# A decoder step's second expert tables: table tiles stationary, tokens moving, and sums that need no turning back

## The chip, the core and the metric

The kernel is one program on one core of a Trainium2 chip. Its time is the device time of one execution in microseconds; the median of several executions is compared. The core has TensorE (matrix products into PSUM), VectorE, ScalarE, GpSimd and the DMA queue of SyncE, each with its own in-order program; they meet through semaphores.

## What is computed

One inference step of a small two-layer decoder, for 256 prompt tokens and 8 x 4 sample tokens, 1024 features. Layer 0 mixes tokens by gated linear attention, layer 1 by a recurrent block. Each is followed by a PEER channel mixer: every token picks 128 of 16384 single-neuron experts (8 heads, top 16 each):

```python
x = x + g1 * mixed
hm = rms_norm(x, p['norm_ffn_g'][i]) * (1 + sc2) + sh2
x = x + g2 * peer_mixer(hm, ...)
...
act = gelu(einsum('thkd,td->thk', u_tab[idx], xb))
wgt = g * act
return einsum('thk,thkd->td', wgt, v_tab[idx])
```

A final norm gives y. Outputs also include the mixers' new states.

## The kernel before

For the prompt tokens the kernel doesn't gather experts. It multiplies with both whole tables, in 128 tiles of 128 experts, and makes the weight of an expert that a token didn't pick zero. Activations lie turned: features on partitions, tokens along the free dimension (`x`, `x2`, `hid`: 128 partitions x 8 feature tiles kk x 288 tokens, the first 256 of the prompt). The 32 sample tokens do gather their rows (`picked`, GpSimd's indirect DMA); their weighted sum `mix_acc` is turned by eight small matmuls (L1469) into bank 3 of `pu`.

Precision comes from splitting each operand into a rounded high and a low part, both fp32r, and adding three products: high x high, high x low, low x high. A table tile comes by DMA from the SyncE queue into one of four slots of `raw`; ScalarE rounds it into `w_hi` (`high`, L814), VectorE (or GpSimd in the U stage) makes `w_lo` (`low`, L1793). `w_hi` and `w_lo` have two buffers each, so the rounding of tile c waits until TensorE is done with tile c-2 (`split_used`). The DMA into a slot waits until the low part that reads it is done.

PEER of a layer has these stages: query projection, scores, routing on VectorE; **U**, the first tables, tile by tile into one of four banks of `pu` (`u_early` for 64 tiles, `u_late` for 64; L1380, L1381, L1385), where a 128x128 piece of the table is the stationary operand and 256 tokens move, 24 matmuls a tile; then **V**, the second tables (`v_four`, L1456 to L1458). In V, ScalarE rounds also the tile's weights of 256 tokens (`weight_high`, L975, into `hid_lo[:, s]`), VectorE makes their low part (`weight_low`, L2085, `hid_lo[:, 4 + s]`).

V before: the weights of 128 tokens are the stationary operand and 512 features of the table move. Two token blocks and two feature halves fill the four banks of `pm`; all 128 tiles add up there. So the result has tokens on partitions, and has to be turned back. Behind the last tile:

```python
for half in range(2):                                # ScalarE; VectorE takes the other banks (L2154)
    act.wait_ge(v_bank, lay * 3 + 2 * half + 1)
    act.activation(v_tok_out[:, 2 * half, :], pm[:, 2 * half, :], ACT.Copy).then_inc(v_evac_act, 1)
```

ScalarE copies banks 0 and 2 (L1041), VectorE banks 1 and 3 (L2154) to `v_tok_out`; TensorE turns them with 16 transposes of 128x128 (L1480) into `pu`; VectorE adds each feature tile, times the layer's gate, to `x2` (L2157) and signals `x_ready`. The sample part of `x` is computed ahead of that (L2146, L2148).

What follows V: in layer 0, ScalarE first rounds the first two weight tiles of the recurrent block's projection (`next_high`, the second waits for V's last tile), then takes squares of the eight tiles of `x` (`square`, L868); VectorE makes the two low parts; GpSimd adds squares in three pairs (0,1), (2,3), (4,5) (`fold_squares`, L596); TensorE sums pairs and the tiles 6 and 7 over partitions with `ones` (`square_sum`, L1263); then come conditioning sums (`gap_sums`, L1281) on TensorE, while the norm is applied elsewhere, and the projection. In layer 1 the squares start at once, and the final norm ends the kernel. Projections take three products in the order hi, hi, lo with 288 moving tokens (`three`, L1243 to L1245).

Of the kernel before, what the change touches and what calls it, by code (L numbers as in the profile page):

```python
# [20 lines left out]
ALU = mybir.AluOpType  # L21
ACT = mybir.ActivationFunctionType
AX_X = mybir.AxisListType.X

P = 128
D = 1024
KD = D // P
SEQ = 256
# [121 lines left out]
def build_step(nc, xt, ct, par, con, ada, gla_in, w_lr, w_gate2, gla_out, wq, keys, u_tab, u_rows, v_tab, rg_in, gates,  # L150
               rg_out, rg_tail, gla_state, h_state, conv_state,
               y_out, gla_p_out, gla_s_out, h_out, conv_p_out, conv_s_out):
    with ExitStack() as ctx:
        def sb(name, shape, dt=F32):
            return ctx.enter_context(nc.sbuf_tensor(name, shape, dt))

        def sem(name):
            return ctx.enter_context(nc.semaphore(name))
# [3 lines left out]
        hid_hi, hid_lo = hid_split[:, 0:KD, :], hid_split[:, KD:2 * KD, :]  # L162
        raw = sb("raw", [P, RING, D])
        w_hi = sb("w_hi", [P, 2, D], F32R)
        w_lo = sb("w_lo", [P, 2, D], F32R)
# [5 lines left out]
        mod = sb("mod", [P, 2, 6, KD, NSEQ])  # L171
# [9 lines left out]
        def area(at, *dims, dt=F32, parts=P):  # L181
            n = 1
            for d in dims:
                n *= d
            v = arena[0:parts, at:at + n]
            if dt != F32:
                v = v.bitcast(dt)
            if len(dims) == 2:
                return v.rearrange("p (a b) -> p a b", a=dims[0])
            if len(dims) == 3:  # L190
                return v.rearrange("p (a b c) -> p a b c", a=dims[0], b=dims[1])
            return v
# [5 lines left out]
        x2 = area(0, KD, T)  # L198
        x = area(34560, KD, T)
# [73 lines left out]
        part_d = [area(27648 + SLOTS * n, SLOTS) for n in range(3)]  # L273
        twice = [w.bitcast(F16).rearrange("p (n d) -> p n d", d=2) for w in part_d]
        pick_u, pick_g, pick_wa, sum4 = [ada_row[:, n * PICKS:n * PICKS + PICKS] for n in range(4)]
        def v_turned(kk):

            return pu[:, kk % 4, kk // 4 * SEQ:kk // 4 * SEQ + SEQ]

        v_tok_out = area(4096, 4, 512)  # L280

        def pcol(name, a=0, b=None):
            lo, hi = PAR_COLS[name]
# [2 lines left out]
        def ccol(name, parts=P):  # L286
            lo, hi = CON_COLS[name]
            return const[0:parts, lo:hi] if hi <= 2 * P else const_gla[0:parts, lo - 2 * P:hi - 2 * P]

        ident, iota = ccol("ident"), ccol("iota")  # L290


        pu = ctx.enter_context(nc.psum_tensor("pu", [P, 4, 512], F32))
        pm = ctx.enter_context(nc.psum_tensor("pm", [P, 4, 512], F32))
# [39 lines left out]
        x_ready = sem("x_ready")  # L334
# [11 lines left out]
        preset = sem("preset")  # L346
        o_turned = [pm[:, 2, :], pm[:, 3, :], pu[:, 2, :], pu[:, 3, :]]
        v_bank = sem("v_bank")
        v_evac_act = sem("v_evac_act")
        v_evac_vec = sem("v_evac_vec")  # L350
        v_turn = sem("v_turn")
        s_mix = sem("s_mix")
        xs_ready = sem("xs_ready")
        picked_in = [sem(f"picked_in{b}") for b in range(GRING)]
# [408 lines left out]
        def _(act):  # L763
# [88 lines left out]
            def root_table(out=mean[:, T - 1:T]):  # L852

                act.activation(out, pcol("final_g", 0, 1), ACT.Abs_reciprocal_sqrt)
# [46 lines left out]
            def peer(lay):  # L901
# [128 lines left out]
                for c in range(NKEY):  # L1030
# [5 lines left out]
                        act.activation(sp[:, 1, :], sp[:, 1, :], ACT.Exp, scale=-1.0).then_inc(lame_ready, 1)  # L1036
                    if c == NKEY - 2:
                        root_table(sel_w[:, 0:1])
                for half in range(2):
                    act.wait_ge(v_bank, lay * 3 + 2 * half + 1)  # L1040
                    act.activation(v_tok_out[:, 2 * half, :], pm[:, 2 * half, :], ACT.Copy).then_inc(v_evac_act, 1)  # L1041


            act.wait_ge(x_in, 16)
# [58 lines left out]
            for j in range(24):  # L1103
# [4 lines left out]
                if j in MIX_ROW:  # L1108
                    g, half = MIX_ROW[j]
# [39 lines left out]
            norm_root(1)  # L1149
            norm_high(1, 0, 3)  # L1150
            peer(0)


# [74 lines left out]
            act.wait_ge(mod_ready, 11)  # L1228
            norm_high(3, 1, 3)
            peer(1)  # L1230
            for kk in range(KD):
                square(4, kk)
# [4 lines left out]
        def _(pe):  # L1237
            mm = pe.matmul

            def three(out, cols, kk, r_hi, r_lo, s, n_k, stop=True):  # L1240
                s2 = s % 2

                mm(out, w_hi[:, s2, cols], r_hi, start=(kk == 0), stop=False)  # L1243
                mm(out, w_hi[:, s2, cols], r_lo, start=False, stop=False)  # L1244
                return mm(out, w_lo[:, s2, cols], r_hi, start=False, stop=(stop and kk == n_k - 1))  # L1245
# [96 lines left out]
            def peer(lay):  # L1342
# [6 lines left out]
                for n in range(9):  # L1349
# [4 lines left out]
                    if n < 8:  # L1354
                        for a in range(4):
                            hp = 4 * (n % 4) + a
                            last = mm(pm[:, n % 4, a * P:a * P + P], qp[:, hp, (n // 4) * P:(n // 4) * P + P], key[:, hp, :],  # L1357
                                      start=True, stop=True)
                    else:
                        for hp in (4 * g + a for a in range(4) for g in range(4)):  # L1360
                            at = hp // 4 * 32
                            last = mm(pm[at:at + 32, 0, (hp % 4) * P:(hp % 4) * P + P], qp[:, hp, SEQ:T], key[:, hp, :],
                                      start=True, stop=True)
# [84 lines left out]
                def v_four(i, first=False, final=False):  # L1448
                    for s in range(4):
                        pe.wait_ge(lo_done, i * 4 + (l0 + NKEY - POOL_ALL + s + 1))  # L1450
                        pe.wait_ge(w_ready, i * 4 + (n0 + s + 1))
                        start, stop = first and s == 0, final and s == 3
                        for bank in range(4):
                            out, cols = pm[:, bank, :], slice(bank // 2 * 512, bank // 2 * 512 + 512)
                            tok = slice(bank % 2 * P, bank % 2 * P + P)
                            mm(out, hid_lo[:, s, tok], w_hi[:, s % 2, cols], start=start, stop=False)  # L1456
                            mm(out, hid_lo[:, 4 + s, tok], w_hi[:, s % 2, cols], start=False, stop=False)  # L1457
                            last = mm(out, hid_lo[:, s, tok], w_lo[:, s % 2, cols], start=False, stop=stop)  # L1458
                            if stop and bank < 3:
                                last.then_inc(v_bank, 1)  # L1460
                        last.then_inc(split_used, 1)

                v_four(0, first=True)
                with pe.Fori(1, NKEY // 4 - 1) as i:
                    v_four(i)
                pe.wait_ge(mix_added, (lay + 1) * (PICKS - 1))
                pe.wait_ge(u_prod, (lay + 1) * LATE)
                for kk in range(KD):
                    last = mm(pu[:, 3, kk * 32:kk * 32 + 32], mix_acc[:, kk * P:kk * P + P], sum4, start=True, stop=True)  # L1469
                last.then_inc(s_mix, 1)  # L1470
                v_four(NKEY // 4 - 1, final=True)
                pe.wait_ge(xs_ready, lay + 1)
                for half in range(2):
                    pe.wait_ge(v_evac_act, 2 * lay + half + 1)
                    pe.wait_ge(v_evac_vec, 2 * lay + half + 1)
                    for a in range(4):
                        if half:
                            pe.wait_ge(x_ready, (2 * lay + 1) * KD + a + 1)
                        for tb in range(2):
                            last = pe.transpose(v_turned(half * 4 + a)[:, tb * P:tb * P + P],  # L1480
                                                v_tok_out[:, half * 2 + tb, a * P:a * P + P], ident)
                        last.then_inc(v_turn, 1)


            pe.wait_ge(ones_set, 1)
# [161 lines left out]
            for j in range(24):  # L1647
# [11 lines left out]
                for kk in range(KD):  # L1659
                    if j == 0:  # L1660
                        pe.wait_ge(hl_ready, kk + 1)
                    last = three(pu[:, j % 2, 0:T], slice(kk * P, kk * P + P), kk, hid_hi[:, kk, :], hid_lo[:, kk, :], j, KD)
# [5 lines left out]
            for c in range(KD):  # L1668
# [3 lines left out]
                for kk in range(KD):  # L1672
                    if c == 0:
                        pe.wait_ge(hl_ready, LOW_BEFORE["gla_out"] + kk + 1)
                    last = three(pu[:, c % 4, 0:T], slice(kk * P, kk * P + P), kk, hid_hi[:, kk, :], hid_lo[:, kk, :], c, KD)
# [12 lines left out]
            for g in (5, 6):  # L1688
                gap_sums(g)
            peer(0)  # L1690


# [49 lines left out]
            for o in range(KD):  # L1742
# [11 lines left out]
                for e in range(2):  # L1754
                    last = mm(pu[:, o % 4, 0:T], tail[:, e, o * P:o * P + P], yb[:, KD + e, :], start=False, stop=(e == 1))
# [5 lines left out]
            pe.wait_ge(mod_ready, 11)  # L1761
            gap_sums(11)
            peer(1)
            pe.wait_ge(ones_set, 3)
            for kk in range(KD):
# [4 lines left out]
        def _(dve):  # L1770
            own = [0]
            tt_, ts, stt = dve.tensor_tensor, dve.tensor_scalar, dve.scalar_tensor_tensor
# [228 lines left out]
            def peer(lay):  # L2001
# [144 lines left out]
                link(tt_(part.rearrange(by_seq, b=NB), pu[:, 3, 0:256].rearrange("p (k b t) -> p k b t", k=KD, b=NB),  # L2146
                         bc(mod[:, lay, 5, :, 1:NSEQ], P, KD, NB, NT), ALU.mult))
                tt_(x[:, :, SEQ:T], x2[:, :, SEQ:T], part, ALU.add).then_inc(xs_ready, 1)  # L2148
                for half in range(2):
                    if half == 0:  # L2150
                        dve.wait_ge(v_bank, lay * 3 + 2)
                    else:
                        dve.wait_ge(split_used, m0 + 2 * NKEY)
                    dve.tensor_copy(v_tok_out[:, 2 * half + 1, :], pm[:, 2 * half + 1, :]).then_inc(v_evac_vec, 1)  # L2154
                for kk in range(KD):
                    dve.wait_ge(v_turn, lay * KD + kk + 1)
                    stt(x[:, kk, 0:SEQ], v_turned(kk), mod[:, lay, 5, kk, 0:1], x2[:, kk, 0:SEQ], ALU.mult,  # L2157
                        ALU.add).then_inc(x_ready, 1)


# [135 lines left out]
            state_sample(5, pm[:, 2:4, :])  # L2296
            out_rows("gla_out", 1, 0, 2)
            peer(0)


# [94 lines left out]
            dve.tensor_copy(hl_out[:, :, 1:NSEQ], samples(g_r)[:, :, :, NT - 1]).then_inc(hs_ready, 1)  # L2395
            out_rows("rg_out", 3, 1, 2)
            peer(1)
            norm_inverse(4)
            for kk in range(KD):
# [94 lines left out]
```

## Time and profile before

| | us |
|---|---|
| median of 3 runs | 2035.35 (2032.27 to 2035.69) |
| profiled execution | 2030.94 |
| its span | 2029.1 |
| TensorE busy, by the records | 1985.0 (98%), 14082 matmuls |
| weight loads on TensorE | 1761.6 (87%) |
| VectorE | 1401.7 (69%) |
| ScalarE | 1254.9 (62%) |
| GpSimd | 846.8 (42%) |

Busy shares are means over the whole span. PE is TensorE's matmuls, PEld its weight loads (they overlap), DVE is VectorE, ACT ScalarE, POOL GpSimd. Matmuls are pipelined and their ends are modelled: the pace of a stream of them is read from the starts. PEclk is the clock granted to TensorE, 1.00 being 2.4 GHz.

### The profile page before, as it was taken

The page shows a single profiled execution, that of the slowest core. Times are in us where ns is not written, and L with a number is a line of the kernel's source. Part 1 is how long each engine was busy: PE and PEld are TensorE (multiplying, and loading weights), DVE is VectorE, ACT ScalarE, POOL GpSimd, SP SyncE. Part 2 cuts the span into 40 slices and gives each one's busy share as a digit, 9 for nine tenths or more (in the row PEclk, how much of TensorE's full clock was granted, in tenths as well). Part 3 has the DMA queues.
Part 4 walks back from the last instruction along what each step waited for, and adds up shares of the span by engine and source line. Part 5 has one row for each costly group of instructions (what it writes and reads, how often), then busy time and mean ns, then how long its engine had stood idle before and what let it go on. Part 6 is the DMA issues. An engine that isn't in the chain of part 4 may idle for free.

```text
span 2029.1 us, 40794 instructions
## 1 busy us (share of the span) xinstructions
PE 1985.0 (98%) x14082; PEld 1761.6 (87%) x14082; DVE 1401.7 (69%) x2784; ACT 1254.9 (62%) x2212; POOL 846.8 (42%) x465
## 2 busy tenths in 40 slices
PE   7999999999999999999999999999999999999998
PEld 4778899999999877777778889999999997777776
DVE  3436569955666777777766754997566667777785
ACT  3544465556777677677654644655677776767774
POOL 0011037885777322234212411888477742223330
PEclk8999999999999999999999999999999999999999
DMA  9847755665455689988947554666655458888883
GB/s 352 294 167 272 266 177 171 186 212 172 155 156 157 204 290 320 351 311 328 326 148 245 166 200 136 186 184 189 198 156 157 157 167 306 297 300 292 301 291 115
DMA packets 125466, 459.54 MB, mean 226 GB/s; under 512 B 14016, under 2 KB 14544, under 8 KB 124352
## 3 DMA queue, kind: packets, MB, share of 16 engines
q1 hardware_dynamic: 103408, 378.71, 56.6%
q0 software_dynamic: 21072, 77.95, 10.5%
q10 hardware_dynamic: 896, 1.76, 0.2%
q8 instruction: 46, 0.75, 0.2%
q14 instruction: 44, 0.36, 0.1%
HBM read 449.93 MB, written 8.44 MB: 226 GB/s over the span
## 4 chain that ended last, share of the span: by engine, by line
PE 91%; DVE 4%; DMA 2%; ACT 1%; issue 1%; SPq 0%; POOL 0%; DVEq 0%; ACTq 0%
PE pu L1385 12%; PE pu L1380 12%; PE pm L1456 12%; PE pm L1458 12%; PE pm L1457 12%; PE pu L1381 12%; PE pu L1243 4%; PE pu L1244 4%; PE pu L1245 4%; PE pm L1415 3%; PE pm L1725 1%; DVE w_lo L1793 1%; DMA arena<-in_ada 1%; DMA raw<-in_gla_out 1%; PE pm L1357 1%; ACT w_hi L814 1%
## 5 line engine op out<-in xcount | busy, mean ns | idle before, releaser
L814 ACT ACTIVATE w_hi<-raw 128x1024 fp32r<-128x1024 f32 x600 | 633.1, 1055 | 410.1 <-PE pm L1458 220.1
L1793 DVE TENSOR_TENSOR w_lo<-raw,w_hi 128x1024 fp32r<-128x1024 f32 x372 | 458.3, 1232 | 365.2 <-ACT w_hi L814 348.9
L1380 PE MATMUL pu<-hid_split,w_hi 128*128 128x256 f32 x2048 | 492.2, 281 | 0.0
L1381 PE MATMUL pu<-hid_split,w_hi 128*128 128x256 f32 x2048 | 491.2, 279 | 0.0
L1456 PE MATMUL pm<-w_hi,hid_split 128*128 128x512 f32 x1024 | 403.9, 394 | 2.6 <-DVE hid_split L2085 2.6
L1458 PE MATMUL pm<-w_lo,hid_split 128*128 128x512 f32 x1024 | 402.3, 393 | 0.0
L1457 PE MATMUL pm<-w_hi,hid_split 128*128 128x512 f32 x1024 | 401.7, 392 | 0.0
L1380 PEld LDWEIGHTS pu<-hid_split,w_hi 128*128 128x128 f32 x2048 | 385.9, 188 | 0.8 <-issue 0.8
L1381 PEld LDWEIGHTS pu<-hid_split,w_hi 128*128 128x128 f32 x2048 | 385.1, 188 | 0.0
L660 POOL TENSOR_TENSOR w_lo<-raw,w_hi 128x1024 fp32r<-128x1024 f32 x128 | 306.4, 2394 | 152.8 <-ACT w_hi L814 152.8
L632 POOL TENSOR_TENSOR w_lo<-raw,w_hi 128x1024 fp32r<-128x1024 f32 x104 | 249.6, 2401 | 169.8 <-ACT w_hi L814 169.8
L1385 PE MATMUL pu<-hid_split,w_lo 128*128 128x256 f32 x2048 | 295.4, 287 | 0.0
L1385 PEld LDWEIGHTS pu<-hid_split,w_lo 128*128 128x128 f32 x2048 | 260.6, 189 | 0.2 <-POOL w_lo L632 0.2
L1456 PEld LDWEIGHTS pm<-w_hi,hid_split 128*128 128x128 f32 x1024 | 192.2, 188 | 70.3 <-issue 19.3
L1243 PE MATMUL pu<-hid_split,w_hi 128*128 128x288 f32 x736 | 227.5, 309 | 13.2 <-DVE w_lo L1793 5.6
L1458 PEld LDWEIGHTS pm<-w_lo,hid_split 128*128 128x128 f32 x1024 | 192.4, 188 | 43.6
L951 ACT ACTIVATE oh_w<-oh_eq,sel_w 128x128 f16<-128x128 f16 x512 | 163.9, 391 | 103.7 <-PE pm L1415 103.7
L1457 PEld LDWEIGHTS pm<-w_hi,hid_split 128*128 128x128 f32 x1024 | 192.7, 188 | 33.4
L1244 PE MATMUL pu<-hid_split,w_hi 128*128 128x288 f32 x736 | 219.7, 299 | 0.0
L1245 PE MATMUL pu<-hid_split,w_lo 128*128 128x288 f32 x736 | 218.9, 297 | 0.0
L647 POOL DMA_INDIRECT arena<-in_v_tab,coef x64 | 110.0, 1719 | 219.5 <-DVE arena L2111 174.4
L647 POOL DMA_INDIRECT arena<-in_u_rows,coef x64 | 76.2, 1191 | 237.4 <-ACT arena L1002 235.9
(283 smaller groups left out, 2559.0 us busy)
## 6 DMA issues: line engine op xcount, KB each, us to landing
raw<-in_u_tab SPq DMA_DIRECT2D x256, 512.0 KB
raw<-in_v_tab SPq DMA_DIRECT2D x256, 512.0 KB
arena<-in_ada SPq DMA_DIRECT2D x56, 512.0 KB, 6.5
raw<-in_wq SPq DMA_DIRECT2D x32, 512.0 KB
raw<-in_gla_in SPq DMA_DIRECT2D x24, 512.0 KB
raw<-in_ada SPq DMA_DIRECT2D x24, 512.0 KB
raw<-in_rg_in SPq DMA_DIRECT2D x20, 512.0 KB
arena<-in_ada SPq DMA_DIRECT2D x8, 1024.0 KB, 16.7
```

The source lines that it names most:

```text
L660: pool.tensor_tensor(w_lo[:, c % 2, :], raw[:, slot, :], w_hi[:, c % 2, :].bitcast(F32), ALU.subtract).then_inc(lo_pool, 1)
L814: act.activation(w_hi[:, s2, :], raw[:, s4, :], ACT.Copy).then_inc(hi_done, 1)
L1243: mm(out, w_hi[:, s2, cols], r_hi, start=(kk == 0), stop=False)
L1244: mm(out, w_hi[:, s2, cols], r_lo, start=False, stop=False)
L1245: return mm(out, w_lo[:, s2, cols], r_hi, start=False, stop=(stop and kk == n_k - 1))
L1380: mm(pu[:, s, 0:SEQ], w_hi[:, s % 2, kk * P:kk * P + P], hid_hi[:, kk, 0:SEQ], start=(kk == 0), stop=False)
L1381: mm(pu[:, s, 0:SEQ], w_hi[:, s % 2, kk * P:kk * P + P], hid_lo[:, kk, 0:SEQ], start=False, stop=False)
L1385: last = mm(pu[:, s, 0:SEQ], w_lo[:, s2, kk * P:kk * P + P], hid_hi[:, kk, 0:SEQ], start=False, stop=(kk == KD - 1))
L1456: mm(out, hid_lo[:, s, tok], w_hi[:, s % 2, cols], start=start, stop=False)
L1457: mm(out, hid_lo[:, 4 + s, tok], w_hi[:, s % 2, cols], start=False, stop=False)
L1458: last = mm(out, hid_lo[:, s, tok], w_lo[:, s % 2, cols], start=False, stop=stop)
L1793: tt_(w_lo[:, s2 if l2 is None else l2, :], raw[:, s4, :], w_hi[:, s2, :].bitcast(F32), ALU.subtract).then_inc(lo_done, 1)
```

## The change

In V the operands change places. A 128x128 piece of the table tile becomes the stationary operand and the 256 tokens' weights move. Each of the eight feature tiles kk has a sum of its own of 128 features x 256 tokens; two of them share a bank of `pm`. Per tile there are 24 matmuls of 256 columns where there were 12 of 512. The first matmul of a bank starts it; the second sum of the bank begins on cleared columns.

The result has features on partitions, as `x` does. `v_tok_out`, its four evictions, the 16 transposes and three semaphores go; VectorE's residual operations read the sums in `pm`: kk 0 to 5 after their bank is complete (`v_bank`), 6 and 7 after the last tile. TensorE's wait for `xs_ready` goes too.

```diff
-        def v_turned(kk):
-            return pu[:, kk % 4, kk // 4 * SEQ:kk // 4 * SEQ + SEQ]
-        v_tok_out = area(4096, 4, 512)
+        def v_sum(kk):
+            return pm[:, kk // 2, kk % 2 * SEQ:kk % 2 * SEQ + SEQ]
...
-                for half in range(2):
-                    act.wait_ge(v_bank, lay * 3 + 2 * half + 1)
-                    act.activation(v_tok_out[:, 2 * half, :], pm[:, 2 * half, :], ACT.Copy).then_inc(v_evac_act, 1)
...
-                        for bank in range(4):
-                            out, cols = pm[:, bank, :], slice(bank // 2 * 512, bank // 2 * 512 + 512)
-                            tok = slice(bank % 2 * P, bank % 2 * P + P)
-                            mm(out, hid_lo[:, s, tok], w_hi[:, s % 2, cols], start=start, stop=False)
-                            mm(out, hid_lo[:, 4 + s, tok], w_hi[:, s % 2, cols], start=False, stop=False)
-                            last = mm(out, hid_lo[:, s, tok], w_lo[:, s % 2, cols], start=False, stop=stop)
-                            if stop and bank < 3:
+                        for kk in range(KD):
+                            out, cols = v_sum(kk), slice(kk * P, kk * P + P)
+                            mm(out, w_hi[:, s % 2, cols], hid_lo[:, s, 0:SEQ], start=(start and kk % 2 == 0), stop=False,
+                               skip_group_check=True)
+                            mm(out, w_hi[:, s % 2, cols], hid_lo[:, 4 + s, 0:SEQ], start=False, stop=False,
+                               skip_group_check=True)
+                            last = mm(out, w_lo[:, s % 2, cols], hid_lo[:, s, 0:SEQ], start=False, stop=stop,
+                                      skip_group_check=True)
+                            if stop and kk in (1, 3, 5):
                                 last.then_inc(v_bank, 1)
                         last.then_inc(split_used, 1)
...
-                pe.wait_ge(xs_ready, lay + 1)
-                for half in range(2):
-                    pe.wait_ge(v_evac_act, 2 * lay + half + 1)
-                    pe.wait_ge(v_evac_vec, 2 * lay + half + 1)
-                    for a in range(4):
-                        if half:
-                            pe.wait_ge(x_ready, (2 * lay + 1) * KD + a + 1)
-                        for tb in range(2):
-                            last = pe.transpose(v_turned(half * 4 + a)[:, tb * P:tb * P + P],
-                                                v_tok_out[:, half * 2 + tb, a * P:a * P + P], ident)
-                        last.then_inc(v_turn, 1)
...
-                for half in range(2):
-                    if half == 0:
-                        dve.wait_ge(v_bank, lay * 3 + 2)
+                for kk in range(KD):
+                    if kk < KD - 2:
+                        dve.wait_ge(v_bank, lay * 3 + kk // 2 + 1)
                     else:
                         dve.wait_ge(split_used, m0 + 2 * NKEY)
-                    dve.tensor_copy(v_tok_out[:, 2 * half + 1, :], pm[:, 2 * half + 1, :]).then_inc(v_evac_vec, 1)
-                for kk in range(KD):
-                    dve.wait_ge(v_turn, lay * KD + kk + 1)
-                    stt(x[:, kk, 0:SEQ], v_turned(kk), mod[:, lay, 5, kk, 0:1], x2[:, kk, 0:SEQ], ALU.mult,
+                    stt(x[:, kk, 0:SEQ], v_sum(kk), mod[:, lay, 5, kk, 0:1], x2[:, kk, 0:SEQ], ALU.mult,
                         ALU.add).then_inc(x_ready, 1)
```

## Rows read from the trace of the kernel before

**Rows 1.** The page: TensorE's busy time, and the chain by engine

```profile
PE 1985.0 (98%) x14082; PEld 1761.6 (87%) x14082; DVE 1401.7 (69%) x2784; ACT 1254.9 (62%) x2212; POOL 846.8 (42%) x465
...
PE 91%; DVE 4%; DMA 2%; ACT 1%; issue 1%; SPq 0%; POOL 0%; DVEq 0%; ACTq 0%
```

**Rows 2.** Windows: length; busy PE, PEld, DVE, ACT, POOL; PEclk, DMA share, GB/s

```profile
684.90:1041.80 356.90, 356.89 (x1554) 284.38 (x1555) 275.41 (x346) 244.08 (x359) 92.46 (x65) 1.00 0.86 305
...
1658.05:2014.80 356.75, 356.74 (x1554) 284.44 (x1555) 271.89 (x323) 242.55 (x355) 89.52 (x62) 1.00 0.80 275
...
1264.00:1439.00 175.00, 175.00 (x1495) 175.00 (x1494) 149.61 (x474) 99.02 (x150) 137.04 (x57) 1.00 0.62 191
```

**Rows 3.** Timeline of PE, layer 0: V's first matmul, its 1488th (start, duration)

```profile
684.91 0.47 PE L1456 MATMUL pm<-w_hi,hid_split 128*128 128x512 f32 x1 [1.31 <-DVE hid_split L2085]
...
1028.50 0.39 PE L1458 MATMUL pm<-w_lo,hid_split 128*128 128x512 f32 x1
```

**Rows 4.** Groups by line: busy us, mean ns of one, then idle before

```profile
L1385 PEld LDWEIGHTS pu<-hid_split,w_lo 128*128 128x128 f32 x2048 | 260.6, 189 | 0.2 <-POOL w_lo L632 0.2
...
L2157 DVE SCALAR_TENSOR_TENSOR arena<-pu,mod,arena 128x256 f32<-128x256 f32 x16 | 6.4, 474 | 0.0
```

**Rows 5.** Timeline of a V tile in layer 0: rounding, low part, first load

```profile
851.30 0.40 PE L1456 MATMUL pm<-w_hi,hid_split 128*128 128x512 f32 x1
...
851.50 1.06 ACT L814 ACTIVATE w_hi<-raw 128x1024 fp32r<-128x1024 f32 x1 [1.44 <-PE pm L1458]
...
852.59 1.23 DVE L1793 TENSOR_TENSOR w_lo<-raw,w_hi 128x1024 fp32r<-128x1024 f32 x1 [0.72 <-ACT w_hi L814]
...
853.94 0.19 PEld L1456 LDWEIGHTS pm<-w_hi,hid_split 128*128 128x128 f32 x1 [0.17 <-issue]
854.03 0.41 PE L1456 MATMUL pm<-w_hi,hid_split 128*128 128x512 f32 x1
```

**Rows 6.** Timeline of PE, U stage of layer 1: first matmuls of tiles 22 apart

```profile
1332.23 0.28 PE L1380 MATMUL pu<-hid_split,w_hi 128*128 128x256 f32 x1
...
1394.12 0.28 PE L1380 MATMUL pu<-hid_split,w_hi 128*128 128x256 f32 x1
```

**Rows 7.** Timeline of PE in the last query projection, 12 matmuls apart

```profile
1229.87 0.30 PE L1243 MATMUL pu<-hid_split,w_hi 128*128 128x288 f32 x1
...
1231.47 0.30 PE L1243 MATMUL pu<-hid_split,w_hi 128*128 128x288 f32 x1
```

**Rows 8.** Timeline of the end of V and what follows, layer 0

```profile
1038.96 0.42 DVE L2148 TENSOR_TENSOR arena<-arena 128x256 f32<-128x256 f32 x1
...
1041.41 0.40 PE L1458 MATMUL pm<-w_lo,hid_split 128*128 128x512 f32 x1
...
1041.63 2.00 ACT L814 ACTIVATE w_hi<-raw 128x1024 fp32r<-128x1024 f32 x2
...
1043.53 2.76 ACT L868 ACTIVATE arena<-arena 128x288 f32<-128x288 f32 x8
...
1044.38 3.28 POOL L596 TENSOR_TENSOR arena<-arena 128x288 f32<-128x288 f32 x3 [6.34 <-ACT arena L868]
...
1047.71 1.72 PE L1263 MATMUL pm<-arena 128*128 128x288 f32 x6 [0.98 <-POOL arena L596]
```

**Rows 9.** Timeline of the end of V and what follows, layer 1

```profile
2014.44 0.39 PE L1458 MATMUL pm<-w_lo,hid_split 128*128 128x512 f32 x1
...
2015.48 3.22 DVE L2157 SCALAR_TENSOR_TENSOR arena<-pu,mod,arena 128x256 f32<-128x256 f32 x8
...
2016.90 2.36 POOL L596 TENSOR_TENSOR arena<-arena 128x288 f32<-128x288 f32 x3 [7.46 <-ACT arena L868]
...
2017.85 3.19 PE L1263 MATMUL pm<-arena 128*128 128x288 f32 x10 [0.23 <-POOL arena L596]
```

**Rows 10.** Timeline of PE in a U tile of layer 1: neighbours

```profile
1357.67 0.27 PE L1381 MATMUL pu<-hid_split,w_hi 128*128 128x256 f32 x1
1357.78 0.28 PE L1380 MATMUL pu<-hid_split,w_hi 128*128 128x256 f32 x1
```

More of the change, by code:

```diff
@@ L348, in build_step @@
         v_bank = sem("v_bank")
-        v_evac_act = sem("v_evac_act")
-        v_evac_vec = sem("v_evac_vec")
-        v_turn = sem("v_turn")
         s_mix = sem("s_mix")
```

## The prediction

> **What bounds the kernel now.** I read the page first. TensorE is busy 98% of the span, and the chain that ended last is 91% TensorE [rows 1]. In such a kernel a change of shape on TensorE counts in full, unless something else already held it there. So I cut the trace into stretches. The two V stages (the second tables) are the ones the change touches: 684.9 to 1041.8 and 1658.05 to 2014.8 us. TensorE is without a gap in both, its granted clock is 1.00 of the upper level (2.4 GHz), while VectorE, ScalarE and the DMA engines have room [rows 2].
>
> Then I looked for the pace. In a V stage 124 of the 128 table tiles run without a break: 1488 matmuls, the first starting at 684.91 and the last at 1028.50 [rows 3]. That is 343.59 us over 1487 steps, 231.1 ns from one 512-column matmul to the next, or 12 x 0.2311 = 2.773 us a tile. The duration beside each (0.47 and 0.39) isn't the pace, since matmuls overlap; only starts count.
>
> Is that pace TensorE's own? The double buffering makes a loop: the end of tile c-2 releases ScalarE's rounding of tile c, then VectorE's low part, then the first weight load. In one tile it reads: ScalarE 851.50, VectorE 852.59 to 853.82, load 853.94, matmul 854.03; the tile before had started at 851.30 [rows 5]. So the loop can't be shorter than 854.03 - 851.30 = 2.73 us a tile, and stands just 0.04 below TensorE's 2.773. TensorE bounds, with the loop close behind.
>
> **Part 1, the matmuls turned round.** Per tile, 12 matmuls of 512 columns with 12 loads become 24 of 256 columns with 24 loads. The columns streamed stay the same, 6144. What counts is what each matmul costs beyond its columns. The U stage of this kernel has nearly the wanted form: 24 matmuls a tile, a 128x128 piece of the table stationary, 256 tokens moving, w_hi twice and w_lo once per piece. From 1332.23 to 1394.12 it does 22 tiles at an even pace [rows 6]: 61.89 / 22 = 2.813 us, 117.2 ns a matmul. Two halves thus cost 234.4 where one whole costs 231.1. In the U stage the loads (188 ns each in the listing, [rows 4]) fill 175.00 of 175.00 us [rows 2], and still the matmuls keep 117.2 ns; so doubling the loads is hidden by the matmuls, for as long as loads go on beside them.
>
> Differences from U: V takes hi, hi, lo piece by piece, and leaves an accumulator after 3 matmuls and a bank after 6, where U does 16 and then 8 into one. Projections have that three-step order with 288 columns: from 1229.87 to 1231.47 there are 12 steps of 133.3 ns [rows 7]. At 2.4 GHz 288 columns are 120.0 ns, so 13.3 are overhead; 256 columns are 106.7, so U's overhead is 10.5. With 13.3 a V matmul would take 120.0 ns, a tile 2.88 us. If I draw a line through U's 256 columns and V's 512 instead, 288 columns would be 131.3 ns; the projections are only 2.0 over it. So the ends are 2.73 (the loop, if TensorE got cheaper) and 2.88 us. I take 2.82: U's pace plus a tenth of the way to the projections', because size and kind of the matmuls are U's. The step per tile is 2.82 - 2.773 = +0.047, over 127 tiles in each of two stages +11.9 us. The ends give -10.9 and +27.2. The loop is now 0.09 below TensorE and hides; SP's loads of table tiles wait for the low parts as before, and DMA moves the same bytes in a longer stage (busy 0.86 and 0.80 of it now [rows 2]).
>
> The Trainium skill (TensorE: Matmul & The Clock Gate, Back-to-back issue gap) has, for isolated matmuls, columns divided by 2.4 GHz plus 2.5 ns; an estimate by it is 24 x 109.2 - 12 x 215.8 = +31 ns a tile, +7.9 us in all. The trace has both a good deal dearer (117.2 and 231.1), with nearly the same difference, so the sum stays with the rows.
>
> **Part 2, the tail behind V.** Out go two ScalarE and two VectorE evictions, 16 transposes and their waits; the eight residual operations (474 ns each when not overlapped in the listing) read the bank sums directly. Six of them have their banks before V is over, 0.7 us apart; VectorE is free there, since its sample sums end at 1039.4 [rows 8]. Only kk 6 and 7 remain behind the last matmul, at about 0.05 and 0.5, ready by 1.0 us.
>
> After layer 1 the modelled end of V is 2014.44 + 0.39 = 2014.83, and the sum of squares is done at 2021.04 [rows 9]: 6.2 us. Afterwards: squares of kk 0 to 5 are done by +0.7, the last at +1.6 (eight take 2.76 in [rows 8]; 0.45 for one alone), GpSimd's third addition (2.36 / 3 = 0.8) at +1.5, then the last three sums on TensorE, 1.72 as in [rows 8]: +3.3. I save 2.9. The bounds: if only the stretch from 2014.83 to the first residual at 2015.48 came out, it were 0.65; if all of the residuals' 3.22 went with it too, 3.9.
>
> After layer 0 less comes free. ScalarE has two roundings of the next weights ahead of its squares, and the second needs the end of V: V + 0.02, 1.06 long. So squares run from about +1.1 rather than from 1043.53 - 1041.80 = +1.73, and this is what is late next. VectorE's two low parts, which run beside GpSimd's additions now (3.28 us for three against 2.36 without them [rows 8, 9]), mostly get out of their way. Additions end at about +4.5 for +5.86, the sums at +6.3 for 1049.43 - 1041.80 = +7.63. I save 1.5, within 0.6 and 2.2. The conditioning sums (gap sums 8 and 9) and the projection follow on TensorE in order and just move.
>
> **Sum.** +11.9 - 2.9 - 1.5 = +7.5 us. On the profiled execution (2030.94 us, span 2029.1, so 1.8 around it) that gives 2038.4. The timed runs stand at 2035.35, 4.4 above the profiled one, and the same step gives 2042.9. Their spread is 3.4 us, so 0.2% (4.1 us) is about what can be told from no change.
>
> **Rivals.**
> *About the same (0.17).* U's pace exactly (+10.2) or a bit under it, and tails at their best ends (-3.9 - 2.2 = -6.1): +4.1 or less, 2035 to 2039. For it: 2.813 is a row of this kernel; against: both must come out well.
> *The three-step order costs as in the projections (0.15).* Accumulator and bank change often and each matmul keeps 13.3 ns over its columns: +27.2 - 4.4 = +22.8, 2058. For it speak rows 7, against it that U differs from them in columns and in order alike.
> *Faster (0.08).* The turned matmuls cost less than U's. In a U tile some steps are only 0.11 us, as from 1357.67 to 1357.78, where both operands change [rows 10], and in V both change at a third of the steps or the destination does. If all 24 took 0.113, TensorE would want 2.71, the rounding loop would hold it at 2.73, and the time would be -10.9 - 4.4 = -15.3, 2020. It decides from under 2.790 us a tile (2.773 + 4.4/254); for a gain over 0.2% the tile must not be dearer than now, 2.774. Against it: all 24 steps average 117.2.
> *Weight loads set the pace (0.02).* Each 188 ns load stands unhidden ahead of its matmul: 24 x 0.188 = 4.51 us of loads alone, +1.74 a tile, +442 us, 2473. It needs that loads don't overlap with matmuls, and in the U stage they plainly do [rows 2, 6]. The same page and section of the Trainium skill says that the spacing in a stream of load and matmul pairs is set by both of them, with 131 ns for 512 columns; that rule speaks against halving the columns, but here 512 columns take 231.1 ns, so the trace doesn't bear its figure out.
>
> **How the numbers follow.** The forecast case has 0.58 and its own range is 2.81 to 2.85 us a tile with the tails' ends: 2038 to 2053. The range reaches down over most of the "same" case to 2034 and up to 2056, under the dear case's centre; outside are about 0.09 below and 0.1 above. A slowdown over 0.2% holds 0.56 of the forecast, and the dear and load cases: 0.73. Within 0.2%: 0.18. Faster: 0.09.
>
> **What would show it.** (a) V matmuls 117 to 119 ns apart, tiles 2.81 to 2.85: right; under 2.79 or over 2.86: my price was wrong. (b) V stages 6 us longer each, in which the idle time of VectorE and ScalarE grows. (c) The low part of a tile ends over 0.3 us ahead of the tile's first matmul; otherwise the loop bounds. (d) The residuals of kk 0 to 5 start before V's last matmul, two after it. (e) Squares' sums at about V's end +6.3 (layer 0) and +3.3 (layer 1). The prediction fails if the step from matmul to matmul depends on order and banks rather than on columns, for 1 ns a matmul is 6.1 us.

## The result, and the profile after

The changed kernel takes 2056.14 us (median of 4 runs, 2055.44 to 2057.37), the kernel before 2033.92, four runs as well: the ratio is 1.0111, interval 1.0097 to 1.0125, or +22.2 us. I had forecast +7.5 and a range up to 2056.0. The direction was right, the size was three times mine, and it ended just outside the range.

The page of the changed kernel, TensorE's busy time:

```profile
PE 2007.4 (98%) x17122; PEld 1929.1 (94%) x17122; DVE 1398.2 (68%) x2780; ACT 1253.2 (61%) x2208; POOL 852.0 (41%) x465
```

The windows of its V stages (columns as in [rows 2]):

```profile
688.80:1057.50 368.70, 368.52 (x3088) 368.35 (x3088) 277.00 (x351) 244.14 (x358) 94.94 (x65) 1.00 0.85 296
...
1675.40:2044.00 368.60, 368.52 (x3088) 368.34 (x3088) 273.40 (x328) 243.12 (x358) 92.37 (x63) 1.00 0.79 267
```

TensorE still has no gap and its clock is 1.00, but loads now fill the stage (368.35 of 368.70; 284.38 of 356.90 in [rows 2]). VectorE and ScalarE are about as busy as before, in a longer stage: they have more slack. So the added time is TensorE's own pace. The loop of rounding and low part isn't what holds it: in layer 0 a tile's low part ends 0.33 to 0.36 us before the tile's first matmul starts, as here (850.60 + 1.23 = 851.83, matmul 852.18).

```profile
850.60 1.23 DVE L1776 TENSOR_TENSOR w_lo<-raw,w_hi 128x1024 fp32r<-128x1024 f32 x1 [1.29 <-issue]
...
852.18 0.28 PE L1447 MATMUL pm<-hid_split,w_hi 128*128 128x256 f32 x1
```

The pace itself, first matmuls of tiles that are 64 apart in layer 0:

```profile
746.23 0.28 PE L1447 MATMUL pm<-hid_split,w_hi 128*128 128x256 f32 x1
...
929.49 0.28 PE L1447 MATMUL pm<-hid_split,w_hi 128*128 128x256 f32 x1
```

That is 183.26 / 64 = 2.863 us a tile, 119.3 ns a matmul, where I had taken 2.82. Now the end of V in both layers, from the timelines:

```profile
1055.31 3.23 DVE L2137 SCALAR_TENSOR_TENSOR arena<-pm,mod,arena 128x256 f32<-128x256 f32 x8 [0.48 <-PE pm L1451]
...
1057.13 0.28 PE L1451 MATMUL pm<-hid_split,w_lo 128*128 128x256 f32 x1
...
1058.41 2.76 ACT L863 ACTIVATE arena<-arena 128x288 f32<-128x288 f32 x8
1058.46 2.35 DVE L1776 TENSOR_TENSOR w_lo<-raw,w_hi 128x1024 fp32r<-128x1024 f32 x2
1059.25 3.84 POOL L591 TENSOR_TENSOR arena<-arena 128x288 f32<-128x288 f32 x3 [5.83 <-ACT arena L863]
...
1061.74 5.14 PE L1255 MATMUL pm<-arena 128*128 128x288 f32 x10 [4.33 <-POOL arena L591]
...
2043.72 0.28 PE L1451 MATMUL pm<-hid_split,w_lo 128*128 128x256 f32 x1
...
2044.28 3.19 PE L1255 MATMUL pm<-arena 128*128 128x288 f32 x10 [0.28 <-POOL arena L591]
```

In layer 1 the sum of squares ends at 2047.47, 3.75 us behind the start of V's last matmul; before it was 2021.04 - 2014.44 = 6.60 [rows 9]. In layer 0 it ends at 1066.88, 9.75 behind; before 1049.43 - 1041.41 = 8.02 [rows 8]. The tail with less work in it became longer. Two windows, the gap and the sums behind it, show one reason:

```profile
1057.40:1061.70 4.30, 0.01 (x1) 0.00 (x0) 3.55 (x6) 3.72 (x9) 2.45 (x2) 0.83 0.73 243
1061.70:1066.90 5.20, 5.16 (x14) 3.25 (x18) 0.00 (x0) 0.00 (x0) 1.40 (x2) 0.50 0.47 164
```

The transposes had stood in that gap. Without them TensorE sits idle for 4.33 us, and the granted clock falls to 0.50, the level of 1.2 GHz: ten records of sums take 5.14 us, for 1.42 + 1.72 before.

The account, from first to last matmul start: V in layer 0 went from 356.50 to 368.24 us, in layer 1 from 356.38 to 368.24, together +23.6; layer 0's tail +1.7; layer 1's tail -2.85. The sum is +22.5, for +22.2 in the medians. (The profiled execution is slower by 4.0 us more, ahead of V, where the code is the same; V begins anywhere from 683.6 to 689.0 in the traces of all kernels here that leave the U stage as it is.)

### The profile page after: what moved, and what is told of

It is laid out like the page before. It is cut to its first block, busy times and chain, and to the rows that moved or that the text cites. A ratio compares the mean times of both kernels' runs of the same rounds, so it can differ in the third digit from the quotient of the medians.

```text
span 2055.6 us, 46862 instructions
## 1 busy us (share of the span) xinstructions
PE 2007.4 (98%) x17122; PEld 1929.1 (94%) x17122; DVE 1398.2 (68%) x2780; ACT 1253.2 (61%) x2208; POOL 852.0 (41%) x465
## 4 chain that ended last, share of the span: by engine, by line
PE 90%; DVE 4%; DMA 3%; ACT 2%; issue 1%; SPq 0%; POOL 0%; DVEq 0%; ACTq 0%
PE pu L1377 12%; PE pm L1447 12%; PE pm L1451 12%; PE pm L1449 12%; PE pu L1372 12%; PE pu L1373 11%; PE pu L1235 4%; PE pu L1236 4%; PE pu L1237 4%; PE pm L1407 3%; PE pm L1708 1%; DVE w_lo L1776 1%; DMA arena<-in_ada 1%; DMA raw<-in_gla_in 1%; DMA raw<-in_gla_out 1%; PE pm L1349 1%
## 5 line engine op out<-in xcount | busy, mean ns | idle before, releaser
L1447 PE MATMUL pm<-hid_split,w_hi 128*128 128x256 f32 x2048 | 578.4, 282 | 2.6 <-DVE hid_split L2068 2.6
L1451 PE MATMUL pm<-hid_split,w_lo 128*128 128x256 f32 x2048 | 577.7, 282 | 0.0
L1449 PE MATMUL pm<-hid_split,w_hi 128*128 128x256 f32 x2048 | 577.7, 282 | 0.0
L1447 PEld LDWEIGHTS pm<-hid_split,w_hi 128*128 128x128 f32 x2048 | 389.0, 190 | 3.0 <-issue 3.0
L1449 PEld LDWEIGHTS pm<-hid_split,w_hi 128*128 128x128 f32 x2048 | 388.6, 190 | 0.0
L1451 PEld LDWEIGHTS pm<-hid_split,w_lo 128*128 128x128 f32 x2048 | 388.4, 190 | 0.0
L642 POOL DMA_INDIRECT arena<-in_v_tab,coef x64 | 114.6, 1791 | 226.0 <-DVE arena L2094 179.1
```

What stands on the lines that cost most here:

```text
L1447: mm(out, w_hi[:, s % 2, cols], hid_lo[:, s, 0:SEQ], start=(start and kk % 2 == 0), stop=False, skip_group_check=True)
L1449: mm(out, w_hi[:, s % 2, cols], hid_lo[:, 4 + s, 0:SEQ], start=False, stop=False, skip_group_check=True)
L1451: last = mm(out, w_lo[:, s % 2, cols], hid_lo[:, s, 0:SEQ], start=False, stop=stop, skip_group_check=True)
```

## The experiments

Unless said otherwise a time is from one profiled execution of each, and the pace is read from the V stage of layer 0: start of a tile's first matmul to that of a tile 64 later. Three things differ between the V matmuls (119.3 ns) and the U matmuls (117.2): order, destination, and what moves. The first four kernels take them, and the DMA traffic, one at a time.

**U's order in V.** All hi products of a tile, then all lo products:

```diff
                             mm(out, w_hi[:, s % 2, cols], hid_lo[:, 4 + s, 0:SEQ], start=False, stop=False,
                                skip_group_check=True)
+                        for kk in range(KD):
+                            out, cols = v_sum(kk), slice(kk * P, kk * P + P)
                             last = mm(out, w_lo[:, s % 2, cols], hid_lo[:, s, 0:SEQ], start=False, stop=stop,
                                       skip_group_check=True)
```

> The changed kernel with the 24 matmuls of a V tile in the order of the U stage: hi, hi for the eight pieces, then lo for the eight. The changed kernel has 119.4 ns from matmul to matmul, the U stage 117.2. Theory A (the order hi, hi, lo, with both operands changing at every third step, costs the 2.2 ns): 117.2 ns here, a tile 2.81 us, about 13 us less than the changed kernel. Theory B (leaving an accumulator and a bank costs): accumulators change oftener here, 16 times a tile, so 119.4 or more. Theory C (the moving operand is freshly written and changes from tile to tile, or other traffic): no change, 119.4.

Measured: 741.62 to 924.88 for 64 tiles, 2.863 us. Not the order. A side finding: here the banks get complete only in the last eight matmuls, so in layer 1 the residuals start at 2038.70 for a last matmul at 2039.09, TensorE waits 1.70 us for the first addition, and its ten records of sums take 4.59 us, for 3.19 in the changed kernel. The clock falls there too (0.73 over 2039.3 to 2045.7), and layer 1's tail is back at 6.6 us.

**One accumulator.**

```diff
-                            out, cols = v_sum(kk), slice(kk * P, kk * P + P)
+                            out, cols = v_sum(kk if first or final else 0), slice(kk * P, kk * P + P)
```

> The changed kernel, but in 120 of 128 V tiles all 24 matmuls add into one 256-column accumulator, so the sums of those tiles are wrong. Theory B (changing accumulators and banks costs the 2.2 ns): 117.2 ns a matmul. Theories A (order) and C (moving operand or traffic): 119.4 as in the changed kernel.

Measured: the V stage takes 368.23 us, as the changed kernel's 368.24. Neither accumulators nor banks matter.

**Other moving operands.** `hid_hi[:, kk]` and `hid_hi[:, (kk + 1) % KD]` in place of the two slots of weights.

> The changed kernel, but in 120 of 128 V tiles the moving operands are the still activations that the U stage streams (high parts, another feature tile at each piece) and not the tile's fresh weights; the sums of those tiles are wrong. Theory C1 (streaming a freshly written operand costs): 117.2 ns a matmul. Theories A, B and C2 (DMA traffic): 119.4.

Measured: 118.8 ns, a stage of 366.63 us. The first of the edits that moves the pace at all, but it doesn't reach 117.2. Both fresh data and the addresses changed here, and either could be what counts.

**Light DMA.** `raw[:, s, 0:256]` is loaded in V instead of the whole slot.

> The changed kernel, but the loads of table tiles in V bring 256 of 1024 columns (the rest of the slot keeps older values, so V's sums are wrong). The DMA engines' busy share in V falls from about 0.85 to 0.3 or less. Theory C2 (the heavier DMA traffic of V, 300 GB/s against 190 in U, costs the 2.2 ns): 117.2 ns or less. Theories A, B, C1: 119.4.

Measured: 368.24 us, to the hundredth. The busy share of DMA fell less than I had expected, to 0.57 (176 GB/s, window 700 to 1020). That is a fall by a third, to below the 0.62 and 191 GB/s of the U stage [rows 2], and it did nothing.

**V's addresses in the U stage.** The clean cross test: U streams `hid_lo[:, s]` and `hid_lo[:, 4 + s]`, which nobody writes there.

```diff
-   mm(pu[:, s, 0:SEQ], w_hi[...], hid_hi[:, kk, 0:SEQ], ...)
-   mm(pu[:, s, 0:SEQ], w_hi[...], hid_lo[:, kk, 0:SEQ], ...)
+   mm(pu[:, s, 0:SEQ], w_hi[...], hid_lo[:, s, 0:SEQ], ...)
+   mm(pu[:, s, 0:SEQ], w_hi[...], hid_lo[:, 4 + s, 0:SEQ], ...)
```

(and `hid_lo[:, s]` with `w_lo`.)

> The changed kernel with the U stage streaming the moving operands by V's addresses (one of four tiles of the low parts for the whole table tile, and one of the next four) in U's order; U's products are wrong. Theory M1 (addresses of the moving operand set the 2.2 ns between U and V): U rises from 117.2 to 119.4 ns, 2.81 to 2.86 us a tile. Theory E (V's surroundings, other engines' work, cost it): U stays at 117.2.

Measured: in its U stage of layer 1 the first matmuls of two tiles 18 apart start at 1366.39 and 1417.93. 51.54 / 18 = 2.863 us: U has taken on V's pace, in its own surroundings, with its own order and traffic, on data written long ago. What sets the difference is which addresses move.

**One moving tile.** All 24 matmuls stream `hid_hi[:, 0]`.

> The changed kernel, but in 120 of 128 V tiles all 24 matmuls stream one and the same activation tile (the sums of those tiles are wrong). With other activations moving the pace had fallen from 119.4 to 118.8 ns, and order, accumulators and DMA traffic had left it at 119.4 exactly. Theory M1 (the pace hangs on which addresses move beside which are loaded): it moves again, by 0.5 ns or more in either direction, and its pattern over the 24 steps differs. Theory E (what remains is other engines' work in the V stage): 118.8 to 119.4 with the pattern kept.

Measured: 744.50 to 928.82, 2.880 us a tile. All 24 steps are 120.0 ns, where the changed kernel has 119.3 on average with steps from 115 to 122. So the pace moved by 0.7 ns and the pattern is gone, as the address theory asked.

**Start addresses.** A slot is 288 floats, 1152 bytes, long: an odd multiple of 128. So slots start at even and odd multiples of 128 bytes by turns, counted from the tensor's start. In the changed kernel's trace the two kinds of tile differ: 2.873 us with even slots, 2.853 with odd. Shifting the 256 weights by 32 floats in every other slot makes all alike:

```diff
+        def w_at(k):
+            return hid_lo[:, k, 32 - 32 * (k % 2):32 - 32 * (k % 2) + SEQ]
```

used by ScalarE, VectorE and TensorE alike (`32 * (k % 2)` for all even).

> The changed kernel with the even slots of the tokens' weights shifted by 128 bytes, so that all eight moving slots begin at an odd multiple of 128 bytes; the result is the reference's. In the changed kernel tiles with even slots take 2.873 us and those with odd slots 2.853. Theory M2 (the start address of the moving operand sets that): all tiles 2.853, 2.5 us less in all. Rival H (the buffer of w_hi and w_lo, which alternates likewise, sets it): 2.873 and 2.853 stay.

> The changed kernel with the odd slots of the tokens' weights shifted by 128 bytes, so that all moving slots begin at an even multiple of 128 bytes from the tensor's start; the result is the reference's. All odd gave 2.848 us a tile for every slot. Theory M2 (the start address of the moving operand): 2.873 to 2.880 for every slot, 119.7 to 120.0 ns a matmul. Rival N (an alternating start is what costs, either uniform layout is cheap): 2.848.

The timelines, 64 tiles apart, all odd and then all even:

```profile
742.69 0.28 PE L1451 MATMUL pm<-hid_split,w_hi 128*128 128x256 f32 x1
...
924.96 0.28 PE L1451 MATMUL pm<-hid_split,w_hi 128*128 128x256 f32 x1
```

```profile
744.37 0.28 PE L1451 MATMUL pm<-hid_split,w_hi 128*128 128x256 f32 x1
...
928.69 0.28 PE L1451 MATMUL pm<-hid_split,w_hi 128*128 128x256 f32 x1
```

2.848 against 2.880 us, each the same for all four slots. The `w_hi` buffers alternate in both, so it isn't they. (The V stages are 366.28 and 370.37 us for the changed kernel's 368.24: all odd saves 3.9 us in both layers together, where I had expected 2.5.) The single moving tile above, `hid_hi[:, 0]`, starts at an even multiple and had the same 120.0 ns.

Still, 118.7 is not 117.2. U alternates both kinds of start, feature tile by feature tile, and does better than either alone. But mixing them is not enough: the kernel with other moving operands mixes them too, within each tile of V (even, odd, even, then odd, even, odd), and has 118.8; its tiles also take 2.844 and 2.856 us by turns, though all stream the same addresses. Which succession of addresses gives U its 117.2 stays open.

**The width.** The larger part is not 119 against 117, but 2 x 119 against 231. First the kernel before with its operands where they were and each matmul cut in two:

```diff
-   mm(out, hid_lo[:, s, tok], w_hi[:, s % 2, cols], ...)          # and the two others
+   for h in range(2):
+       o, cc = pm[:, bank, h * 256:h * 256 + 256], slice(cols.start + h * 256, cols.start + h * 256 + 256)
+       mm(o, hid_lo[:, s, tok], w_hi[:, s % 2, cc], ...)          # and the two others
```

> The kernel before, tokens stationary and its tail unchanged, with each 512-column matmul of V cut into two of 256 columns with a load each; the result is the reference's. Theory W (the width alone is the cost: half the columns, double the instructions and loads): 117 to 119.5 ns a matmul, the whole kernel 2035 + 10 to 23, as the changed kernel's V. Theory R (the changed roles of the operands cost): the pace stays at 231.1 / 2 = 115.6 ns, the time at 2035.

Measured: 742.72 to 925.75, 2.860 us a tile (119.2 ns), and 2054.95 us for the kernel, 22.6 over the 2032.34 of the kernel before beside it. Nothing was turned round here, and nearly the whole loss is there: the V stages take 367.81 us each, +22.7 in both layers together, for +23.6 in the changed kernel. Cutting a matmul in two also doubles the loads. No kernel here keeps one load for two halves, so what follows calls the two together the cost of the narrow matmul.

The other way: turned round, but with wide matmuls. The weights' high and low parts move together as 512 columns, 16 matmuls a tile.

```diff
+   both = hid_lo.rearrange("p (a b) t -> p b a t", a=2)[:, s, :, 0:SEQ]
+   mm(pm[:, kk // 2, :].rearrange("p (a t) -> p a t", a=2), w_hi[:, s % 2, cols], both, ...)
```

> The changed kernel, but in 120 of 128 V tiles the two products with the high table part are one 512-column matmul that streams the weights' high and low parts together, into a whole bank, so neighbouring sums mix and V is wrong: 16 matmuls and 16 loads a tile for 24, the same 6144 columns, the table still stationary. Theory W (a half-width matmul costs 3.8 ns more than half of a whole one): 231 + 119 ns per piece, a tile 2.80 us. Theory R (the table as the stationary operand costs, whatever the width): 2.86 us.

```profile
800.07 0.40 PE L1454 MATMUL pm<-hid_split,w_hi 128*128 128x512 f32 x1
800.31 0.28 PE L1456 MATMUL pm<-hid_split,w_lo 128*128 128x256 f32 x1
800.42 0.40 PE L1454 MATMUL pm<-hid_split,w_hi 128*128 128x512 f32 x1
```

Over 120 tiles a piece takes 232.8 + 118.8 ns and a tile 2.813 us: eight matmuls fewer, 51 ns less. The roles of the operands cost next to nothing (119.3 ns turned, 119.2 not turned), the narrow matmuls do.

**Narrower still**, 192 tokens in the inner tiles:

> The changed kernel, but in 120 of 128 V tiles only 192 of the 256 tokens move, so 64 tokens lack those tiles. Theory L (the stream of weight loads sets 119.4 ns, the columns hide behind it): still about 119 ns a matmul. Theory M (a matmul costs its columns at 2.4 GHz plus a fixed overhead of 12.7 ns): 80.0 + 12.7 = 92.7 ns, a tile 2.22 us, until ScalarE and VectorE bound it at 2.73 us a tile; then the matmuls within a tile still show 93.

Two neighbours within a tile are 112 ns apart, not 93. The window 700 to 1000 has the loads over the whole of it:

```profile
700.00:1000.00 300.00, 299.93 (x2663) 299.76 (x2662) 240.91 (x284) 216.63 (x316) 87.79 (x61) 1.00 0.92 330
```

A quarter fewer columns saved 7.3 of 119.3 ns where one column a cycle of 2.4 GHz would have saved 26.7. So at 192 columns something other than the columns sets the pace of a pair of load and matmul, and holds it at 112 ns. By the same estimate of one column a cycle, 256 columns (106.7 ns) pay 12.6 ns over their columns, or 25 for two, where 512 columns (213.3) pay 17.8. That 112 ns is a floor, near which 256 columns begin to pay, is my reading of these three widths; fewer than 192 columns weren't tried. (Tiles are 2.703 us there, 0.015 over 24 x 112 ns: the first step of a tile is 136 ns on average, the loop of rounding and low part showing, forecast at 2.73.) The Trainium skill (TensorE: Matmul & The Clock Gate, LDWEIGHTS (loading the stationary operand)) gives a load its columns divided by 1.2, an estimate of 107 ns for 128; the 112 ns from pair to pair lie close to it, but the record of one load in the changed kernel is 186 to 192 ns long, loads overlap, and these runs don't separate the load from other costs of a pair.

**The tail: clock.** 32 transposes of a constant on TensorE ahead of layer 0's sums.

```diff
+            for n in range(32):
+                pe.transpose(pu[:, n % 2, 0:P], ident, ident)
             pe.wait_ge(ones_set, 2)
```

> The changed kernel with 32 transposes of a constant on TensorE between layer 0's V and the sums of squares, where the 16 transposes stood before. In the changed kernel TensorE is idle there for 4.3 us, its granted clock is 0.50 behind it, and its ten records of sums take 5.14 us (1.42 + 1.72 with the clock at 1.00 before). Theory K (the idle time let the clock fall, and that ate the tail's gain): clock 1.00, the sums' end at about 7 us behind V's last matmul instead of 9.7, the kernel 2 to 3 us shorter there. Rival G (GpSimd's additions, 3.84 us for 3.28, are what is late, the clock is not the cause): the end moves by under 0.7 us.

```profile
1056.49 3.13 PE L1255 MATMUL pm<-arena 128*128 128x288 f32 x10 [0.83 <-POOL arena L591]
```

The clock is 1.00 over 1051.9 to 1059.6, and the sums end at 1059.62, 7.74 us behind the start of V's last matmul (1051.88), for 9.75. Theory K holds for 2.0 us. It only gives back what was lost: the tail before took 8.02.

**The tail: VectorE beside GpSimd.** In addition, the two low parts wait for the three additions (`dve.wait_ge(sq_added, FOLD_BEFORE[2] + 3)` ahead of `next_low`).

> The changed kernel with the 32 transposes of the warm-tail experiment, and VectorE's two low parts of the next weights moved behind GpSimd's three additions in layer 0. With the clock held at 1.00 the sums still ended 7.7 us behind V's last matmul, and the additions took 3.83 us, the first 2.4. Theory G (VectorE's low parts beside GpSimd's additions hold the first one up): three additions in 2.4 to 2.8 us, sums' end at 6.3 to 6.7 us behind the last matmul. Rival S (ScalarE's squares pace the additions): 3.8 us and 7.7 stay.

```profile
1057.21 0.28 PE L1451 MATMUL pm<-hid_split,w_lo 128*128 128x256 f32 x1
...
1059.35 2.31 POOL L591 TENSOR_TENSOR arena<-arena 128x288 f32<-128x288 f32 x3 [5.84 <-ACT arena L863]
...
1060.83 2.60 PE L1255 MATMUL pm<-arena 128*128 128x288 f32 x10
1061.68 2.36 DVE L1778 TENSOR_TENSOR w_lo<-raw,w_hi 128x1024 fp32r<-128x1024 f32 x2 [3.06 <-POOL arena L591]
```

The additions take 2.31 us for 3.83, and the sums end 6.22 behind the last matmul's start. Theory G holds for another 1.5 us. The next projection on TensorE starts 13.17 us behind V's last matmul, for 16.81 in the changed kernel and 14.97 before. (The whole kernels, one run each, took 2050.97 us with the transposes and 2054.26 with both; single runs differ by more than the 1.5 us.)

**The kernel before with aligned slots.** If start addresses matter for what moves, they may for what is loaded. Before, even slots had tiles of 2.740 and odd ones of 2.799 us. The same shift, on the kernel before:

> The kernel before with the odd slots of the tokens' weights shifted by 128 bytes, so that all stationary operands begin at even multiples; the result is the reference's. Before, tiles with even slots take 2.740 us and those with odd slots 2.799. Theory M2 (the address of the stationary operand matters as well): all tiles 2.74, -7.5 us, 0.37% faster than before. Rival H (the w buffers alternate, or the loop of rounding and low part makes long and short tiles by turns): no change within 0.2%.

> The kernel before with the even slots shifted by 128 bytes, so that all its stationary operands begin at an odd multiple; the result is the reference's. All even gave 2.755 us a tile and 0.2% less time. Theory M2 (the stationary operand's address): 2.78 to 2.80 us a tile, 2 to 7 us more than before. Rival N (alternating is what costs): 2.755, 4 us less than before.

Measured, 64 tiles apart: 741.51 to 917.73 all even, 741.88 to 920.62 all odd. That is 2.753 against 2.793 us a tile, around the 2.773 of the mixture. The all-even kernel takes 2028.96 us (median of 11 runs) against 2033.52 for the kernel before (15 runs), ratio 0.9980, interval 0.9971 to 0.9989. The all-odd kernel, one run, takes 2039.71 against 2034.24, +5.5. The all-even one is the only version here with the reference's result that beats both kernels, by 4.6 us over the kernel before. The size I had expected (7.5 us, 2.74 a tile) came out at 60%. The likely reason is the loop of rounding and low part: with all slots even the low part ends 0.23 us ahead of the tile's first matmul, with all odd 0.28. That was not tried by itself.

There is a limit to this reading. The halved kernel above loads the same slots, but moves 256 columns, and there it is the other way round: its tiles with even slots take 2.880 us and those with odd slots 2.840. So which start is the better one for the loaded operand seems to turn with the width of what moves; the `w_hi` buffer alternates with the slot in the halved kernel too, and no run separates the two.

## Why the prediction was right and wrong

- *TensorE bounds V, and its pace counts in full:* right. +23.6 us came in V, VectorE and ScalarE gained slack, and the low parts end 0.33 to 0.36 us ahead of the tile's first matmul, over the 0.3 that sign (c) asked for.
- *The loads are hidden:* only in part. They don't stand ahead of each matmul (the load rival's +442 us), but at 192 columns a pair of load and matmul still takes 112 ns, and two matmuls of 256 columns pay 25 ns over their columns where one of 512 pays 17.8. Whether load or matmul asks for that isn't shown.
- *The price of a turned matmul* is the step that failed: "I take 2.82: U's pace plus a tenth of the way to the projections', because size and kind of the matmuls are U's." It measured 2.864 over the 124 tiles that gave 2.773 before. The +11.9 of the sum should have been +23 (254 tiles x 0.091; the stages measured +23.6). That narrow matmuls cost it, and not the turned roles, is shown by the halved kernel, whose V costs nearly as much. Of the +23, U's pace alone would be +10.2. The rest is which addresses move: with V's moving addresses U takes 2.863 as well. The part of it that the start at odd or even multiples of 128 bytes explains is smaller, 118.7 to 120.0 ns; why U's own succession of addresses gives 117.2 isn't known. Size and kind were U's; the addresses weren't, and I had not looked why U's own 24 steps are unequal.
- *The dear rival:* its size was nearly right (+22.8), its mechanism wrong. U's order gave the same 2.863. It was a mere bound from [rows 7] that happened to lie close, and I gave it 0.15.
- *Layer 1's tail, -2.9:* right, -2.85.
- *Layer 0's tail, -1.5:* wrong in sign, +1.7. Two covers were gone that I had costed at nothing. The transposes held the granted clock up (2.0 us), and VectorE's low parts, which by my forecast "mostly get out of their way" beside GpSimd's additions, came to lie over the first of them (1.5 us). With both mended the tail ends at +5.94 behind V's modelled end, for +6.3 forecast, so the forecast's fault was these two covers and not the rest of its chain.
- *The residuals of kk 0 to 5 start before V's end:* right, from 1055.31, 1.8 us ahead of the last matmul.

The expected gain of the change, a shorter tail, was there in layer 1 alone and was outweighed eight times by the pace of 6144 half-width matmuls.

## What to carry to other kernels

Before halving the width of a stream of matmuls, take the price of the narrow form from a stage that has it, and then ask what differs there besides order and size: where the operands start. Here 1 ns a matmul was 6 us. A list of steps within one tile, and of tiles by buffer slot, can show such a cost before any experiment: the kernel before had 2.740 and 2.799 us by turns in V. And work that is taken out of a gap on TensorE may have been holding its clock up: price the gap that it leaves, and see which engines now meet in it.

## What I had not expected of the hardware

- The start address of an operand changes the pace of matmuls. Moving operand of 256 fp32r columns, the loaded one always at even multiples: 118.7 ns with all starts at odd multiples of 128 bytes from the tensor's start, 120.0 at even ones. Loaded operand, with 512 moving columns at even multiples: 229.4 ns (2.753 / 12) at even, 232.7 at odd multiples. Loaded operand with 256 moving columns (the halved kernel): 120.0 at even, 118.3 at odd; the `w_hi` buffer alternates with the slot there and wasn't separated. I know no cause, and offsets other than 128 bytes weren't tried.
- A pair of load and matmul takes 112 ns with 192 columns at the full clock, where 256 take 119.3.
- TensorE idle for 4.33 us was followed by sums at the granted clock 0.50, 5.14 us for about 3.1. In the U-order kernel 1.70 us of waiting at the end were followed by 4.59 for 3.19. With 32 transposes of a constant in the gap the clock stayed at 1.00.
- GpSimd's three additions take 2.31 us alone, and 3.84 when two of VectorE's 1024-column subtractions (2.35 us, not slowed) begin ahead of the first.
